# The order of the small attention products in a decoder kernel's branch turns

## The reference

```python
proj = x @ w_in + b_in                      # 2048 -> 10240
q, k, v, u, q_mem, gate_logits = split(proj)
sb  = stick_breaking(q, k, v)               # 8 heads of 128
y   = s5(u)                                 # 32 groups, 64 complex states each
ssm = glu(gelu(y))
mm  = softmax_attention(q_mem, mem @ w_kv)  # 4 heads of 128, 256 memory tokens
merged = g0 * (sb @ w_sb) + g1 * (ssm @ w_ssm) + g2 * (mm @ w_mem)
x = layer_norm(alpha * x + merged @ w_o)
x = layer_norm(alpha * x + (silu(x @ w_gate) * (x @ w_up)) @ w_down)
```

## Time and profile before

| | us |
|---|---|
| median of 3 runs | 2997.2 |
| lowest and highest | 2996.66, 2997.71 |
| the profiled execution: its time | 2996.06 |
| the profiled execution: its span | 2994.3 |
| PE busy | 2956.2 |
| DVE busy | 2046.1 |
| ACT busy | 1480.6 |
| POOL busy | 137.7 |

### The profile page before, as it was taken

The page is one execution under the profiler, slowest core; times in us unless marked ns, Lnnn a source line. Parts: engine busy times, 40 slices in busy tenths (PEclk is TensorE's granted clock), DMA queues, the critical chain, the costliest instruction groups (busy, mean ns, idle before and its releaser), DMA issues.

```text
span 2994.3 us, 46594 instructions
## 1 busy us (share of the span) xinstructions
PE 2956.2 (99%) x16222; PEld 2537.1 (85%) x16222; DVE 2046.1 (68%) x3168; ACT 1480.6 (49%) x2004; POOL 137.7 (5%) x179
## 2 busy tenths in 40 slices
PE   7999999999999999999999999999999999999999
PEld 6888888888888888888888888888878888888887
DVE  6899866665766655655699996666668556555666
ACT  5666545544544444444465665545435444444443
POOL 6000011110000000000000001111100000000000
PEclk9999999999999999999999999999999999999999
DMA  9656666665555555555556566766655555555554
GB/s 283 174 156 165 168 191 187 190 188 208 216 197 190 194 196 184 181 195 196 185 143 170 160 171 184 194 182 191 214 198 183 197 187 180 194 196 188 190 185 152
DMA packets 673764, 561.76 MB, mean 188 GB/s; under 512 B 20904, under 2 KB 637456, under 8 KB 673168
## 3 DMA queue, kind: packets, MB, share of 16 engines
q1 hardware_dynamic: 669904, 548.48, 59.5%
q10 hardware_dynamic: 3776, 12.21, 1.1%
HBM read 552.52 MB, written 8.13 MB: 187 GB/s over the span
## 4 chain that ended last, share of the span: by engine, by line
PE 93%; DVE 4%; SPq 1%; issue 1%; ACT 1%; DMA 0%; DVEq 0%; ACTq 0%
PE banks L1672 22%; PE banks L1657 22%; PE banks L1674 11%; PE banks L1660 11%; PE banks L1682 7%; PE banks L1683 7%; PE banks L1684 7%; PE banks L1989 2%; DVE lo L1098 1%; PE banks L1991 1%; DVE st L1306 0%; SPq L404 0%; SPq L375 0%; PE banks L1843 0%; SPq L386 0%
## 5 line engine op out<-in xcount | busy, mean ns | idle before, releaser
L1098 DVE TENSOR_TENSOR lo<-raw,hi 128x1024 fp32r<-128x1024 f32 x1016 | 1213.5, 1230 | 434.6 <-ACT hi L659 397.7
L659 ACT ACTIVATE hi<-raw 128x1024 fp32r<-128x1024 f32 x884 | 906.2, 1054 | 547.1 <-PE banks L1674 290.9
L1672 PE MATMUL banks<-xs,hi 128*128 128x512 f32 x2880 | 910.8, 398 | 4.9 <-DVE xs L1234 3.6
L1657 PE MATMUL banks<-xs,hi 128*128 128x512 f32 x2496 | 792.4, 399 | 4.7 <-issue 3.4
L1674 PEld LDWEIGHTS banks<-xs,lo 128*128 128x128 f32 x2880 | 541.8, 188 | 127.4
L1674 PE MATMUL banks<-xs,lo 128*128 128x256 f32 x2880 | 567.2, 278 | 0.0
L1660 PEld LDWEIGHTS banks<-xs,lo 128*128 128x128 f32 x2496 | 470.0, 188 | 110.8
L1660 PE MATMUL banks<-xs,lo 128*128 128x256 f32 x2496 | 491.9, 279 | 0.0
L1672 PEld LDWEIGHTS banks<-xs,hi 128*128 128x128 f32 x2880 | 440.8, 189 | 8.9 <-DVE xs L1234 5.4
L1657 PEld LDWEIGHTS banks<-xs,hi 128*128 128x128 f32 x2496 | 381.8, 189 | 11.1 <-issue 9.8
L1682 PE MATMUL banks<-hi,hT 128*128 128x512 f32 x704 | 274.2, 389 | 0.0
(11 more groups left out here) (224 smaller groups left out, 2664.1 us busy)
## 6 DMA issues: line engine op xcount, KB each, us to landing
raw<-in_ffn_w_gate_up SPq DMA_DIRECT2D x176, 1024.0 KB, 5.0
raw<-in_w_in SPq DMA_DIRECT2D x156, 1024.0 KB, 5.7
raw<-in_ffn_w_down SPq DMA_DIRECT2D x88, 1024.0 KB, 5.2
raw<-in_w_o SPq DMA_DIRECT2D x32, 1024.0 KB, 5.2
raw<-in_sb_w_out SPq DMA_DIRECT2D x32, 512.0 KB, 4.1
raw<-in_mem_w_kv SPq DMA_DIRECT2D x12, 1024.0 KB, 5.6
raw<-in_ssm_w_out SPq DMA_DIRECT2D x32, 256.0 KB, 4.5
raw<-in_mem_w_out SPq DMA_DIRECT2D x32, 256.0 KB, 4.7
```

Source lines behind the costliest of these rows:

```text
L659: act.activation(hi[:, hl_slot(ph, c, h), :], raw[:, slot, h * HALF:(h + 1) * HALF], ACT.Copy).then_inc(hi_ready, 1)
L1098: dve.tensor_tensor(lo[:, s, :], raw[:, slot, h * HALF:(h + 1) * HALF], hi[:, s, :].bitcast(F32), ALU.subtract).then_inc(lo_ready, 1)
L1657: pe.matmul(dst[:, :], hi[:, s, k * P:(k + 1) * P], x_t[:, k0 + k, :], start=first and k == 0, stop=False)
L1672: pe.matmul(bank[base + j], hi[:, s, at[j]], x_t[:, k, :], start=k == 0, stop=False)
```

## The change

PE: the attention product of the first head (`attend(0)`) moves from behind product 4 to behind product 5. The transposes of the memory's v, with their wait for `pt_copied`, move from there to directly behind the first head's transposes and sums, ahead of product 4. ACT: the copy of the memory's v moves up behind the copy of the first v; `tile(5)` now stands ahead of `out_hi(0)`. DVE: `out_lo(0)` moves from ahead of `tile(5)` to behind the scan step that follows it, directly ahead of `softplus(1)`. Nothing is added or removed. This holds for all eight turns.

```diff
--- before.py
+++ after.py
@@ -927,6 +927,7 @@
                     split(4)
                     weights(0)
                     copy_v(0, VO, v_s, 3)
+                    copy_v(1, S, vm_s, 2)
                     if first:
                         table(7)
                     tile(4, turn * 2 + 9)
@@ -936,9 +937,8 @@
                             act.wait_ge(tab_saved[q], 32 if q < 2 else 16)
                         act.wait_ge(bu_done, n * 4 + 4)
                         load_tables(n + 1, 0, tab_b_full)
+                    tile(5, turn * 2 + 17)
                     out_hi(0, VO, sbT[:, bass.ds(turn * 2, 1), 0:T])
-                    copy_v(1, S, vm_s, 2)
-                    tile(5, turn * 2 + 17)
                     softplus(1)
                     if last:
                         split_next("GLU", l, 0, 0)
@@ -1449,10 +1449,10 @@
                     tile(4, k_f)
                     split(5)
                     scan_states(1, 2, 4)
-                    out_lo(0, VO, part_of(sbT, turn * 2, 1), part_of(sbT, turn * 2, 0))
                     dve.wait_ge(vt_done, n * 3 + 4)
                     tile(5, v_f)
                     scan_states(1, 4, 5)
+                    out_lo(0, VO, part_of(sbT, turn * 2, 1), part_of(sbT, turn * 2, 0))
                     softplus(1)
                     if last:
                         split_next("GLU", l, 0, 0)
@@ -1924,13 +1924,13 @@
                     got(2)
                     v_turn(0, v_f, VO)
                     tri(0)
+                    pe.wait_ge(pt_copied, n + 2)
+                    v_turn(1, vm_f, S)
                     half(4, xs, 0)
                     first_table(7)
                     half(4, xs, 1)
+                    gemm(5, xs)
                     attend(0)
-                    pe.wait_ge(pt_copied, n + 2)
-                    v_turn(1, vm_f, S)
-                    gemm(5, xs)
                     pe.wait_ge(v_copied, n * 3 + 3)
                     for mt in range(2):
                         ins = pe.matmul(S[:, T:2 * T], vm_s[:, mt, :], probT[:, mt, :], start=mt == 0, stop=mt == 1)
```

## The result

The changed kernel takes 3037.55 us (median of 4 runs, 3035.99 to 3039.5), the kernel before 2996.93 us in the same comparison: 1.0136 times as long, interval 1.0124 to 1.0147. The prediction was 2997.0 us with a range of 2995.0 to 2999.2. It is wrong by 40 us, and on the side to which it gave 3 in 100. One of the 22 executions of the kernel before with which e5 to e8 are compared took 7112.86 us; no ratio counts it.

What follows compares the result with a forecast made beforehand. TensorE's own work was taken to bound the kernel; PE's reordering gave 0.24 us less, ACT, DVE and moved waits 0, so 2996.06 became 2995.8 us, or 2997.0 us carried to the median, range 2995.0 to 2999.2.

Steps and rivals of the forecast that it cites:

- the side to which it gave 3 in 100: Whole kernel: the outcome of being slower by over 0.2%, given a chance of 0.03.
- the paragraph on the moved waits: PE, memory's v transposes ahead of product 4: their wait for copied probabilities is met 1.66 us before asked for; cost 0.
- The term at 0: PE: the cost forecast for the waits that move with the memory's v transposes, 0 us.
- The paragraph on ACT: ACT: the memory's v copy fits a 2.24 us gap, the attention output's copy has 0.87 us of cover; cost 0.
- The list of PE's waits: PE, profile before: longest total read as 4.4 us in three places, with none of the moved lines in it.
- The sum of PE's own steps: PE, first v transpose to memory product: 13.10 us against 13.13, 0.03 less a turn, 0.24 us less in all.
- The bounds of -1.9 and +1.6 us: PE's reordered products: best case 1.9 us less in all, worst case 1.6 us more.
- ACT at no cost behind product 5: ACT behind product 5: bias step first, then attention output, with 0.87 us of cover before softplus; cost 0.
- DVE at no cost: DVE: attention output's low part moves directly ahead of softplus, output 1.6 us later, 1.7 us left before PE asks; cost 0.
- The rival of the held product 4: PE ahead of product 4: memory's transposes held by the probabilities' copy, 6.7 us lost, 3003.9 us; chance 0.03.
- The late instructions: DVE issue idling and 1.19 us of PE idle behind it: 1.2 us less or 2.4 us more; chance 0.08 together.
- The Trainium skill's rule on weight loads: PE: a load takes columns divided by 1.2 ns, 107 ns for 128; by it the gain is 0 instead of 0.24 us.

Runs made afterwards that it cites:

- e5: Changed kernel with 8 idle 512-column matmuls ahead of the memory's v transposes in each turn: 3029.41 us, ratio 1.0106.
- e8: Kernel before with only the attention product moved on PE behind product 5, ACT and DVE keeping their old lists: 3004.90 us, ratio 1.0027.
- e3: Changed kernel in full new order, but the memory's v transposes wait for the copies of the turn before: 2996.85 us, ratio 1.0002.
- e1: Changed kernel with the memory's v transposes and their waits put back between products 4 and 5: 2997.01 us, ratio 1.0002.
- e2: Kernel before with only the memory's v transposes moved ahead of product 4 and their ACT copy behind the first v copy: 3040.18 us, ratio 1.0142.
- e4: Changed kernel with 16 idle 512-column matmuls ahead of the memory's v transposes in each turn: 3027.49 us, ratio 1.0101.
- e7: Changed kernel with the memory's v transposes and their waits between the two halves of product 4: 3006.72 us, ratio 1.0031.

## Why the prediction was wrong

The step that failed is the paragraph on the moved waits, which ends in "Cost: 0". It checked one wait of the transposes (`pt_copied`, met 1.66 us early) and left out the other, `v_copied`. The description of the kernel ahead of the prediction takes that one for a wait for the previous copy of the memory's v; its threshold asks for this turn's first v as well. The term at 0 measured 31.0 us, and the low clock behind it, which had no term at all, 10.7 us. The paragraph on ACT has the same gap: it looked at when the copy of the memory's v could *run*, not at what the transposes ask of the copy ahead of it.

The price could have been read from the rows that were already there. ACT's copy of the first v ran from 160.17 to 160.55. The memory's transposes asked for it at 163.13, 2.6 us later, so no wait of theirs showed in the profile before. They stood directly behind `attend(0)`, which needs the same copy, and so their own wait could not hold PE at all there. In the new place PE asks at 156.66 + 0.22 = 156.88: 3.67 us too early. The step measured in that turn is 3.92 us, 3.70 more than 0.22. The first turn of layer 0, where ACT has table copies ahead of the split, can be read in the same way from the kernel before (PE, then ACT):

```profile
90.44 0.39 PE L1864 MATMUL banks<-sp_t,ntri 128*128 128x128 f32 x2
95.18 0.38 ACT L868 ACTIVATE v_s<-banks 128x256 f32<-128x256 f32 x1
```

PE would ask at 90.44 + 0.22 = 90.66, and the copy ends at 95.56: 4.90 us too early. With 7 x 3.67 for the others that is 30.6 us; measured, 31.0. A wait that never showed had its cover of 2.6 us in product 4, and the move of 6.25 us took that and more.

The other steps, one by one:
- The list of PE's waits was misread: "the longest total is 4.4 us" holds for its third row only. The first two are 6.5 us (L1727) and 4.9 us (L1802), before as after. None of the moved lines is in it, so nothing followed from the slip.
- The sum of PE's own steps, 13.10 us: right to 0.02 in six turns (13.12 in e3, where nothing else was changed but the wait), but with the third turn the sign of the small total came out the other way. The bounds of -1.9 and +1.6 us for this were wider than needed.
- ACT at no cost behind product 5, DVE at no cost: right (e1: ratio 1.0002). DVE's timeline after has the output's low part behind the scan step, as forecast.
- The rival of the held product 4: right in place and form (PE stands ahead of product 4 on something of ACT's), wrong in the producer. It was priced from the copy L922, with a point of decision at 1.66 us, where the true one had been passed by 3.67 us.
- That PE at 2.4 GHz stays there was not argued at all: every term was a duration at full clock. 10 of the 40 us are that omission. The trace before has a case of it: PE was idle for most of 45.5 to 51.7 us, the last 3.4 us of that being the longest wait in the row, and then worked at half clock:

```profile
52.00:54.00 2.00, 2.00 (x7) 1.61 (x7) 1.68 (x3) 1.37 (x2) 1.75 (x4) 0.50 0.85 366
```

- The late instructions: the 1.2 us of PE idle at L1915 were there again after, unchanged.
- The Trainium skill's rule on weight loads, as the prediction cites it, decided nothing. By it the gain would have been 0, and the 13.12 us of e3 lie 0.01 below before's 13.13, nearer to 0 than to my 0.03, but the rows are rounded to 0.01; on the whole kernel neither can be told from the other.

No version beats the kernel before by an amount that can be told. The full new order with the older copies' wait (e3) is level with it.

## What to carry to other kernels

When a step that waits (a consumer) moves ahead in its engine's list, work out the threshold of every semaphore that it waits on, with the counter's starting value, for one concrete turn. Then compare the time at which the producer ends in the trace with the time at which the consumer will *now* ask. A profile of before names only the waits that hold an engine up; one with 2.6 us of cover is invisible and was worth 31 us here. And where a move adds idle time to a saturated TensorE, allow for slower work behind each idle stretch: here 1.3 to 1.6 us in seven of eight turns, and in e2 up to 2.3 (7.94 against 5.67).

## What the runs showed of the hardware

In the changed kernel, idle stretches of 3.3 to 3.6 us on PE inside dense work were followed by a granted clock of about half in six of the seven turns that had them, and so was one of 4.9 us in the first turn of layer 0. In that same turn so were 3.0 us (e5) and 2.1 us (e7), but not 1.1 us (e4). The 3.62 us in the first turn of layer 1 were not, nor were the 3.62 us in the third turn of layer 1 in e2, where the clock did fall in the first (0.68 as the mean of 3 us), nor were the idle stretches of e5 in the other seven turns, 1.5 to 1.8 us each. So the length alone did not decide it in these runs: two stretches of 3.62 us left the clock full, and one of 2.1 us did not. What else does is open. That filling the wait with useless matmuls is worth 10 us, as e4 showed, I had expected only after the changed kernel's profile.
